# The end of the first block's mixer: another tile order for the pair of output strips, the second strip two tiles behind, pooling moved ahead of attention's last products

## The reference, cut to what matters

```python
def first_block(x, ...):                      # SEQ = 512 tokens, D_MODEL = 1024, two layers
    for l in range(DEPTH):
        h = rms_norm(x, norm_mix_pre[l])
        proj = h @ w_in[l]
        q_da, k_da, v_da, q_r, k_r, v_r, g_r, u_pool = jnp.split(proj, split_points, axis=-1)
        o_da = diff_attention(q_da, k_da, v_da, ...)          # 4 heads of 128: rms_norm of each head at its end
        o_ret = retention(q_r, k_r, v_r, g_r, ret_norm[l])    # 256 wide, gated: silu(g) * o
        o_pool = pool_mixer(u_pool, pool_w[l], pool_scale[l]) # 256 wide: window means, then 64x64 products
        mix = jnp.concatenate([o_da, o_ret, o_pool], axis=-1) @ w_out[l]
        x = x + rms_norm(mix, norm_mix_post[l])
        h = rms_norm(x, norm_mlp_pre[l])
        x = x + rms_norm(conv_mlp(h, ...), norm_mlp_post[l])
    return x

def reference(x, ...):
    return second_block(first_block(x, ...), ...)
```

## Time and profile before

| what | us |
|---|---|
| median of 3 runs (3868.41 to 3869.09) | 3869.07 |
| the profiled execution's own time | 3868.8 |
| its span in the trace | 3867.0 |
| TensorE busy | 3706.8 (96%) |
| VectorE busy | 2460.2 (64%) |
| ScalarE busy | 1570.5 (41%) |
| GpSimd busy | 808.0 (21%) |

### The profile page before, as it was taken

The page is one execution under the profiler, slowest core; times in us unless marked ns, Lnnn a source line. Parts: engine busy times, 40 slices in busy tenths (PEclk is TensorE's granted clock), DMA queues, the critical chain, the costliest instruction groups (busy, mean ns, idle before and its releaser), DMA issues.

```text
span 3867.0 us, 63923 instructions
## 1 busy us (share of the span) xinstructions
PE 3706.8 (96%) x24602; PEld 3359.1 (87%) x24602; DVE 2460.2 (64%) x3404; ACT 1570.5 (41%) x2691; POOL 808.0 (21%) x711
## 2 busy tenths in 40 slices
PE   8989999998999989999999989998999999998998
PEld 5766888686788789998998989998999899898998
DVE  4657763675776386773447576768677444758667
ACT  3534332353433254453233454445445323445444
POOL 1111110111111042320002043325332000305232
PEclk9999999999999999999999999999999999999999
DMA  3112233212222322322110222322233112022223
GB/s 112 48 58 76 93 99 104 77 45 65 71 98 96 103 80 94 103 94 74 55 61 23 75 87 94 104 94 87 96 103 105 66 50 66 12 88 82 99 99 104
DMA packets 106051, 313.30 MB, mean 81 GB/s; under 512 B 29920, under 2 KB 30048, under 8 KB 105536
## 3 DMA queue, kind: packets, MB, share of 16 engines
q1 hardware_dynamic: 105232, 304.60, 23.9%
q0 software_dynamic: 560, 5.09, 0.4%
HBM read 307.48 MB, written 2.10 MB: 80 GB/s over the span
## 4 chain that ended last, share of the span: by engine, by line
PE 86%; issue 6%; DVE 4%; ACT 2%; POOL 2%; DMA 0%; SPq 0%; DVEq 0%; POOLq 0%; ACTq 0%
PE acc L2456 34%; PE misc L2901 22%; PE acc L2922 13%; PE acc L2546 4%; PE misc L3263 1%; PE acc L2880 1%; DVE t_lo L1762 1%; PE acc L3245 1%; PE misc L2475 1%; PE misc L2456 1%; PE acc L2975 1%; PE misc L3080 1%; POOL probs_hi L2281 1%; PE acc L2529 1%; PE misc L3055 1%
## 5 line engine op out<-in xcount | busy, mean ns | idle before, releaser
L624 ACT CAST w_hi<-stage 128x1024 fp32r<-128x1024 f32 x312 | 325.4, 1044 | 834.0 <-PE acc L2456 709.8
L2456 PE MATMUL acc<-x_hi,w_hi 128*128 128x264 f32 (+1 forms) x2112 | 593.1, 333 | 32.5 <-DVE w_lo L1317 10.4
L2456 PE MATMUL acc<-x_lo,w_hi 128*128 128x264 f32 (+1 forms) x2112 | 586.0, 330 | 0.0
L2456 PE MATMUL acc<-x_hi,w_lo 128*128 128x264 f32 (+1 forms) x2112 | 583.8, 329 | 0.0
L1317 DVE TENSOR_TENSOR w_lo<-stage,w_hi 128x1024 fp32r<-128x1024 f32 x312 | 422.9, 1355 | 214.0 <-ACT w_hi L624 204.8
L1747 DVE TENSOR_TENSOR w_lo<-stage,w_hi 128x512 fp32r<-128x512 f32 (+1 forms) x432 | 363.9, 844 | 164.5 <-ACT w_hi L947 161.1
L2456 PEld LDWEIGHTS acc<-x_hi,w_hi 128*128 128x128 f32 x2112 | 361.8, 193 | 82.9 <-issue 22.5
L947 ACT CAST w_hi<-stage 128x512 fp32r<-128x512 f32 (+1 forms) x432 | 261.0, 605 | 344.8 <-PE acc L2922 293.7
L2456 PEld LDWEIGHTS acc<-x_lo,w_hi 128*128 128x128 f32 x2112 | 361.3, 193 | 33.8
L2456 PEld LDWEIGHTS acc<-x_hi,w_lo 128*128 128x128 f32 x2112 | 361.1, 193 | 32.9
L2901 PE MATMUL misc<-t_hi,w_hi 128*128 128x264 f32 x1280 | 366.1, 286 | 0.0
(11 more groups left out here) (390 smaller groups left out, 8094.0 us busy)
## 6 DMA issues: line engine op xcount, KB each, us to landing
stage<-weights SPq DMA_DIRECT2D x568, 512.0 KB, 3.3
rotary_decay<-tables POOLq DMA_DIRECT2D x2, 2048.0 KB, 8.4
x<-x_in SPq DMA_DIRECT2D x4, 512.0 KB, 7.9
lse_rows<-lse_columns SPq DMA_DIRECT2D x128, 0.5 KB, 2.0
out<-x SPq DMA_DIRECT2D x8, 256.0 KB, 2.1
rotary_masks<-tables SPq DMA_DIRECT2D x2, 784.0 KB, 4.4
params<-params SPq DMA_DIRECT2D x2, 279.0 KB, 3.9
consts<-consts POOLq DMA_DIRECT2D x1, 529.0 KB, 4.9
```

Of the source, the lines that this page charges most:

```text
L624: nc.scalar.copy(whi[p][:, :], stage[p][:, :]).then_inc(hi_ready, 1)
L2456: ins = mm(ps[:, b, 0:tn], ww, act_[:, kt, t0:t0 + tn], start=start and n == 0 and q == 0, stop=stop and n == last and q == 2)
```

## The change

It touches the order of work at this one place, and no arithmetic: the same tiles, products and splits are made. `order1()` becomes (0, 1, 6, 7, 2, 4, 5, 3). ScalarE's and VectorE's calls follow the new order, and the parts of tiles 0, 1 and 6 move up between head 3's last probabilities. VectorE's two window means move up to the place behind `lse(3, 1)`, and `head_norm(2)` moves up by two instructions. The pool products move up before `second_half`. In the pair the second strip now follows two tiles behind the first, and `head_square(3)` stands inside the pair, behind the fourth round. The first strip ends with its eighth tile instead of waiting for the second strip's seven.

```diff
-            return (4, 5, 6, 7, 0, 1, 2, 3)
+            return (0, 1, 6, 7, 2, 4, 5, 3)
...
                 two(probs, 3, 4)
-                two(probs, 3, 6)
                 ev.up(IN1)
                 act.wait_ge(evacuated, ev.now())
+                for h in range(2):
+                    act.wait_ge(o1_norm, at(4, h + 1))
+                    hi_of(xh[:, h, 0:SEQ], PV[:, h, :])
+                act.wait_ge(pool_full, at(2, 1))
+                hi_of(xh[:, 6, 0:SEQ], s1_bank(0), gain(C_PSC, 0))
+                two(probs, 3, 6)
+                act.wait_ge(pool_full, at(2, 2))
+                hi_of(xh[:, 7, 0:SEQ], s1_bank(1), gain(C_PSC, 1))
+                act.wait_ge(o1_norm, at(4, 3))
+                hi_of(xh[:, 2, 0:SEQ], PV[:, 2, :])
                 for m in range(2):
                     nc.scalar.activation(RC[:, m, :], PR[:, 4 + m, :], ACT.Tanh, scale=0.5).then_inc(silu_ready, 1)
+                out_square(3)
                 logs_and_exps()
                 for m in range(2):
                     act.wait_ge(gated_ready, at(2, m + 1))
                     hi_of(xh[:, 4 + m, 0:SEQ], PR[:, 2 + m, :], 0.5)
-                for m in range(2):
-                    act.wait_ge(pool_full, at(2, m + 1))
-                    hi_of(xh[:, 6 + m, 0:SEQ], s1_bank(m), gain(C_PSC, m))
-                for h in range(3):
-                    act.wait_ge(o1_norm, at(4, h + 1))
-                    hi_of(xh[:, h, 0:SEQ], PV[:, h, :])
-                out_square(3)
                 out_inverse(3)
...
                 lse(3, 1)
+                window_mean(0)
+                window_mean(1)
                 two(probs_lo, 3, 0)
                 split_lo()
+                head_norm(2)
                 two(probs_lo, 3, 2)
                 strip_out(PR[:, 5, :])
                 half_out(3)
                 two(probs_lo, 3, 4)
                 split_lo()
-                head_norm(2)
+                part_lo(0, xl[:, 0, 0:SEQ], PV[:, 0, :], xh[:, 0, 0:SEQ].bitcast(F32))
                 two(probs_lo, 3, 6)
-                window_mean(0)
-                window_mean(1)
+                part_lo(1, xl[:, 1, 0:SEQ], PV[:, 1, :], xh[:, 1, 0:SEQ].bitcast(F32))
                 head_out(3)
+                for m in range(2):
+                    part_lo(2 + m, xl[:, 6 + m, 0:SEQ], s1_bank(m), xh[:, 6 + m, 0:SEQ].bitcast(F32), gain(C_PSC, m))
+                part_lo(4, xl[:, 2, 0:SEQ], PV[:, 2, :], xh[:, 2, 0:SEQ].bitcast(F32))
                 ret_gate(0)
                 ret_gate(1)
...
                 values_and_scores(3, 0)
-                second_half(s1)
-                values_and_scores(3, 2)
-                values_and_scores(3, 4)
-                two(values, 3, 6)
                 pe.wait_ge(s1_exp, at(32, 32))
...
+                second_half(s1)
+                values_and_scores(3, 2)
+                values_and_scores(3, 4)
+                two(values, 3, 6)
...
+                for n in range(KT):
+                    pe.wait_ge(ml_ready, at(8, n + 1))
+                    tile(0, n)
+                    if n >= lag:
+                        tile(1, n - lag)
+                    if n == 3:
+                        pe.wait_ge(o1_sq, at(4, 4))
+                        pe.wait_ge(o1_ln, at(4, 3))
+                        mm(M[:, 3, :], ones128, sq[:, 1, 0:SEQ], start=True, stop=True).then_inc(o1_var, 1)
+                for n in range(KT - lag, KT):
+                    tile(1, n)
```

More of the change, by code:

```diff
@@ L1643, in mixer1 @@
                 for m in range(2):
-                    part_lo(m, xl[:, 4 + m, 0:SEQ], PR[:, 2 + m, :], xh[:, 4 + m, 0:SEQ].bitcast(F32), 0.5)
-                for m in range(2):
-                    part_lo(2 + m, xl[:, 6 + m, 0:SEQ], s1_bank(m), xh[:, 6 + m, 0:SEQ].bitcast(F32), gain(C_PSC, m))
-                for h in range(3):
-                    part_lo(4 + h, xl[:, h, 0:SEQ], PV[:, h, :], xh[:, h, 0:SEQ].bitcast(F32))
+                    part_lo(5 + m, xl[:, 4 + m, 0:SEQ], PR[:, 2 + m, :], xh[:, 4 + m, 0:SEQ].bitcast(F32), 0.5)
                 head_norm(3)
@@ L2826, in out_pair, with tile @@
                     slots.append(next_slot())
-                    for tile in order1()[0:7]:
-                        if k == 0:
-                            ready += 1
-                            pe.wait_ge(ml_ready, at(8, ready))
-                        half_strip((strip[0] + k) % 2, slots[k], [tile], "middle" if tile != 4 else "first")
-                pe.wait_ge(ml_ready, at(8, 8))
-                for k in range(2):
-                    half_strip(strip[0] % 2, slots[k], [3], "last").then_inc(strip_done, 1)
-                    strip[0] += 1
+                def tile(k, n):
+                    order = "first" if n == 0 else "last" if n == KT - 1 else "middle"
+                    ins = half_strip((strip[0] + k) % 2, slots[k], [order1()[n]], order)
+                    if n == KT - 1:
+                        ins.then_inc(strip_done, 1)
+                for n in range(KT):
[9 more added lines that the diff above has]
+                    tile(1, n)
+                strip[0] += 2
             def layer1():
```

3 lines of the change are left out of this document (1 added, 2 removed).

## The result

The median fell from 3869.08 us (runs of 3868.41, 3869.07, 3869.09 and 3874.40) to 3836.57 us (3832.73, 3834.05, 3839.09 and 3844.22). The ratio is 0.9917, with a 95% interval of 0.9901 to 0.9933, so the changed kernel is 32.5 us faster. The profiled execution took 3839.1 us with a span of 3837.3.

What follows compares the result with a forecast made beforehand. TensorE bounds the kernel (86% of the chain that ended last), through its holes and lower-clock stretches. Savings of 10.5 + 9.8 + 3.4 = 23.7 us from 3868.8 give 3845.1, a median of 3845.4; range 3841.5 to 3850.5.

Steps and rivals of the forecast that it cites:

- third strip, with wait: Output projection's third strip, first layer: starts at 245.6 instead of 256.06 after a 1.1 us TensorE wait, saving 10.5 us.
- clock behind the pair: Behind the pair: no slow stretch follows the shorter wait, so 1.7 us a layer go, 3.4 us saved.
- The sum: Savings of both layers and the clock behind them: 10.5 + 9.8 + 3.4 = 23.7 us.
- The means: VectorE's window means in its 2.60 us hole ahead of 215.61: take 2.64 us, delaying the probabilities' remainder 0.1 us.
- The named cover: TensorE asks for the remainder of probabilities only behind a half strip ending about 217.5, so its delay costs nothing.
- The table switch: ScalarE, attention's end to retention's tiles: load alone; the opposing rule puts about 2.8 us more ahead of the logarithm.
- rival B: Tile 3's chain late, by slow parts or two-load switches (about 2.3 us a layer): 3850.0, at worst 3851.8; chance 0.10.
- A: Lower clock stays behind the third strip's wait or head 3's waits: 1.7 us a layer, 3848.8; chance 0.13.
- C: Waits in the interleaved pair add up to 8 us a layer, slow stretches return: saving under 7.7 us; chance 0.04.
- D: TensorE from 219.62 to the third strip stays at 1.2 GHz: +9 us a layer, 3887; chance 0.03.
- the pool bound: Range allowance for the pool products' cost, taken as 1.9 us between 1.8 and 2.2: -0.2, +0.6 for both layers.
- the tile waits: Range allowance for a tenth here and there in TensorE's waits for tiles: 1 us either way.

Runs made afterwards that it cites:

- the first profile: The changed kernel profiled in the session of the result: span 3837.3 us, 61.4 us of lost clock in 23 stretches.
- the 18 later runs: The changed kernel, unaltered, timed six times in each of three further sessions: mean 3845.5 us, session ratios 0.9940, 0.9937 and 0.9943.
- the 63 of before: Runs of the kernel before the change, in the same sessions as the changed kernel's later runs: mean 3869.2 us.
- first repeat: The changed kernel, unaltered, profiled again and timed six times: mean 3845.0 us, ratio 0.9940; profile span 3838.0 us.

## Why the prediction was right and wrong

Corrected times are those of the first profile less 0.56 us.

| step | forecast | corrected | verdict |
|---|---|---|---|
| pool products push the half strip by | 1.9 | 1.96 | right |
| exponential ahead of the last ones starts | 229.2 | 229.36 | right |
| the pair starts | 231.9 | 231.99 | right |
| tile 6, with wait | 233.5 (0.2) | 233.66 | 0.2 late |
| square, and its time | 236.3 (1.0) | 236.56 (1.02) | right, and at full clock |
| logarithm on ScalarE | 238.2 | 238.09 | right |
| tile 3, last | 241.7 | 241.66 | right |
| third strip, with wait | 245.6 (1.1) | 245.66 (0.94) | right |
| second layer saves | 9.8 | 9.67 | right |
| clock behind the pair | 1.00 | 1.00 in both layers | right |

**The sum** was 23.7 us, and the place gave 23.5. Over the 18 later runs and the 63 of before beside them the gain is 23.7, and their mean of 3845.5 is the forecast time; that both agree to 0.1 us is luck, since the mean of 18 such runs is itself uncertain by 1 us. The prediction's reading of the waits at this place and of the lower clock behind them is thus shown by the trace, and by the runs with one part undone: fillers in the waits remove the slow square and the slow stretch, the interleaving alone removes the second of them, the order alone leaves it.

**The means** were a step whose sum was right and whose size was off. VectorE's timeline of the changed kernel:

```profile
213.69 0.86 DVE L1475 TENSOR_SCALAR ret_scores<-ret_scores,consts 128x496 f32<-128x496 f32 x1
...
215.39 0.48 DVE L1475 TENSOR_SCALAR retention_pool<-retention_pool,consts 128x496 f32<-128x496 f32 x1
215.91 0.98 DVE L1476 TENSOR_TENSOR retention_pool<-retention_pool 128x512 f32<-128x512 f32 x1
216.81 1.45 DVE L1446 TENSOR_TENSOR probs_lo<-probs,probs_hi 128x512 fp32r<-128x512 f32 x2
```

They took 3.3 us (213.49 to 216.81) and not 2.64, and the remainder of probabilities came 0.64 us late (corrected 216.25 for 215.61) instead of 0.1. The named cover held: its value products did not move. The cause lies on GpSimd, below.

**The table switch**, on which a rule of the Trainium skill spoke against the change. ScalarE's timeline of the changed kernel:

```profile
231.59 0.63 ACT L695 ACTIVATE x_hi<-v_then_out 128x512 fp32r<-128x512 f32 x1
232.24 1.28 ACT L873 ACT_TABLE_LOAD   x1
233.53 1.15 ACT L873 ACTIVATE rot_cos<-retention_pool 128x512 f32<-128x512 f32 x2
...
235.22 1.28 ACT L637 ACT_TABLE_LOAD   x1
236.79 0.63 ACT L695 ACTIVATE x_hi<-retention_pool 128x512 fp32r<-128x512 f32 x1 [0.28 <-DVE retention_pool L1488]
238.65 0.67 ACT L766 ACTIVATE squares<-misc,eps_and_one 128x512 f32<-128x512 f32 x1
```

The load begins 0.02 us behind the part and the `Tanh` 1.29 us behind the load's start. Behind the second load the next activation is held by VectorE's gate for 0.28 us, and not by the switch. The Trainium skill (ScalarE: Activation LUTs, What ACT_TABLE_LOAD costs) adds 1380 ns of drain to every switch; the trace shows none here, and the second of rival B's mechanisms, switches that hold ScalarE for two load rows, is refuted with it.

**Rivals A, B, C and D** did not come about: the clock behind the pair is 1.00, tile 3 is on time, the largest wait within the pair is 0.2 us, and the whole stretch runs at the full clock.

**What failed** is the step on the clock in the rest of the program. The sum has no term for it, and the range reached down to 3841.5 for the case that "slow stretches elsewhere happen to fall better with everything 12 and 24 us earlier (one of them is 1.7)". Of the 3.9 us between 3845.4 and 3841.5 the pool bound and the tile waits have 1.2, so this term was given 2.7 us, and only as luck on one side. The windows over the whole span show 70.0 us of such stretches before, and in the profile of the result 61.4: 8.6 us less, of which 6.2 came through to the span, where the prediction had 2.7 at most. In the four profiles of the changed kernel they are 61.4 to 76.8, in 23 to 28 pieces, and single runs of one program scatter by 9 to 17 us in a session with them. I had taken one profile and three runs within 0.7 us as the measure of how far the rest of the program repeats.

Two things are to be kept apart here. With the scatter that the later runs show, a mean of four runs is uncertain by some 2 us, and twice that below 3841.5 is 3837.5; a range that wide is what the record now asks for, and 3836.6 lies below even this. That the first session's mean lies 8.0 us under that of the other 18 runs is more than such scatter. Its runs' clocks say how the time was saved, not why there: why the two fastest runs had a mean clock of 0.985 stays open, and no experiment here reaches it.

## What to carry to other kernels

Where the busiest engine stands still for a join of several branches, put ahead those operands that are ready long before, and let the second consumer run some steps behind the first: the order was worth 7.5 us in a layer and the lag 2.9 on top of it, and neither cost an instruction. The wait of 2.3 us ahead of the third strip was paid twice, as itself and as 1.7 us of lower clock behind it, so cutting it to 0.9 gave 3.1 us a layer and not 1.4. Before you put a range around a forecast, sum the time at the lower clock over the whole span, not only at the edit: where it is 2% of the time and scattered over two dozen places, runs of the same program differ by more than a small edit is worth.

## What the runs showed of the hardware

**The lower clock follows some waits, and it also comes without one.** Waits of 2.32 and 2.33 us ahead of the third output strip were followed by a slow stretch in every profile that had them (six waits in three profiles), and waits of 0.24 to 0.95 us ahead of the same strip by none (18 waits in nine profiles). But the size of a wait does not settle it elsewhere. This is one strip in the second block, TensorE's timeline and a window of the changed kernel's first profile:

```profile
2229.23 0.48 PE L2460 MATMUL acc<-x_hi,w_hi 128*128 128x264 f32 x2 [2.46 <-DVE w_lo L1320]
```

```profile
2229.00:2237.00 8.00, 7.77 (x64) 7.80 (x65) 7.97 (x9) 6.86 (x20) 7.76 (x7) 1.00 0.40 133
```

and of its first repeat:

```profile
2228.23 0.48 PE L2460 MATMUL acc<-x_hi,w_hi 128*128 128x264 f32 x2 [2.29 <-DVE w_lo L1320]
```

```profile
2229.00:2237.00 8.00, 8.00 (x55) 8.00 (x54) 8.00 (x8) 6.46 (x19) 7.84 (x8) 0.79 0.38 133
```

The longer wait left the clock at 1.00, and the shorter one was followed by a stretch that cost 1.7 us. And the stretches from 1868 to 1978 and from 3117 to 3221 in the kernel before begin with TensorE busy. A profile shows one draw of all this.

**VectorE and GpSimd slow each other.** The two tensor_scalar rows above are one operation on the same shape. The one at 213.69 took 0.86 us and the one at 215.39 took 0.48, and the tensor_tensor at 215.91 took 0.98 where the one at 214.58 took 0.69. GpSimd's timeline of the changed kernel in that stretch:

```profile
213.66 0.60 POOL L2264 COPY retention_pool<-retention_pool 64x512 f32<-64x512 f32 x1 [0.17 <-POOL retention_pool L2264]
215.53 1.73 POOL L2285 CAST probs_hi<-probs 128x512 fp32r<-128x512 f32 x2 [1.26 <-ACT probs L758]
```

The same operations in the kernel before, on VectorE with GpSimd idle, and on GpSimd:

```profile
229.50 0.48 DVE L1472 TENSOR_SCALAR ret_scores<-ret_scores,consts 128x496 f32<-128x496 f32 x1
```

```profile
214.96 1.06 POOL L2281 CAST probs_hi<-probs 128x512 fp32r<-128x512 f32 x2 [1.24 <-ACT probs L758]
```

The two slow rows of VectorE began while GpSimd's copy or cast ran. The row at 215.39 began 0.14 us ahead of the cast and kept its 0.48. The two casts took 1.73 us here and 1.06 us in the kernel before, where VectorE stood idle until 215.61. The two slow rows are 0.38 and 0.29 us over the same rows of the kernel before, which makes the 0.67 us between 2.64 and 3.3, and all eight profiles with the means in this place have them. The Trainium skill (GPSIMD Engine Reference, 1. Specifications) says that the two engines share their interfaces to the on-chip memory and contend for some kinds of VectorE instruction, and the trace agrees. Whoever moves VectorE's work into one of its holes should see whether the hole is one in which GpSimd works: it was here, and the 2.64 us became 3.3.
